# The order of VectorE's two groups of sums in the seven-product down projection

## The reference

```python
D_FF = 4 * D_MODEL          # 4096, D_MODEL = 1024, SEQ = 512, DEPTH = 2
h = rms_norm(x, g_mlp_pre)
f = jnp.square(jax.nn.relu(h @ w_up)) @ w_down
return x + rms_norm(f, g_mlp_post)
```

## Time and profile before

| | us |
|---|---|
| median of three runs | 2084.41 |
| lowest and highest | 2078.05, 2085.26 |
| the profiled execution's own time | 2079.13 |
| its span in the profile | 2077.0 |

### The profile page before, as it was taken

The page is one execution under the profiler, slowest core; times in us unless marked ns, Lnnn a source line. Parts: engine busy times, 40 slices in busy tenths (PEclk is TensorE's granted clock), DMA queues, the critical chain, the costliest instruction groups (busy, mean ns, idle before and its releaser), DMA issues.

```text
span 2077.0 us, 28000 instructions
## 1 busy us (share of the span) xinstructions
PE 2027.3 (98%) x10072; PEld 1626.9 (78%) x10072; DVE 1330.8 (64%) x1979; ACT 942.2 (45%) x1385; POOL 943.6 (45%) x368
## 2 busy tenths in 40 slices
PE   8999999999999999999999998999999999999999
PEld 7875888888888776888888886768776887888887
DVE  5866257787757654278778758884688624464555
ACT  6345464444453446543444452355576443333332
POOL 5433246544546233764666565224221353443442
PEclk9999999999999999999999999999999999999999
DMA  5432223333325331232333332232211332233222
GB/s 188 155 112 79 64 63 101 112 109 101 101 71 171 122 92 41 64 110 90 101 102 120 102 134 88 72 102 92 82 41 61 122 94 80 91 101 101 88 94 81
DMA packets 111854, 202.24 MB, mean 97 GB/s; under 512 B 6544, under 2 KB 51856, under 8 KB 111504
## 3 DMA queue, kind: packets, MB, share of 16 engines
q1 hardware_dynamic: 104800, 189.12, 28.2%
q10 hardware_dynamic: 6960, 11.88, 2.0%
HBM read 189.44 MB, written 8.12 MB: 95 GB/s over the span
## 4 chain that ended last, share of the span: by engine, by line
PE 73%; issue 16%; DVE 6%; POOL 4%; ACT 1%; DMA 0%; ACTq 0%; DVEq 0%; POOLq 0%
PE bank L800 40%; PE bank L1047 13%; PE bank L1027 7%; PE bank L914 5%; POOL w_lo L606 3%; PE bank L1058 2%; PE bank L925 1%; PE bank L872 1%; PE bank L983 1%; PE bank L943 1%; PE bank L971 1%; DVE partner L2728 0%; DVE w L2685 0%; POOL sums L622 0%; DVE pr L2299 0%
## 5 line engine op out<-in xcount | busy, mean ns | idle before, releaser
L606 POOL TENSOR_TENSOR w_lo<-raw,w_hi 128x2048 fp32r<-128x2048 f32 (+1 forms) x123 | 540.7, 4396 | 840.3 <-ACT w_hi L1547 825.8
L800 PE MATMUL bank<-act_hi,w_hi 128*128 128x512 f32 x1072 | 428.3, 400 | 5.2 <-POOL w_lo L606 2.7
L800 PE MATMUL bank<-act_hi,w_lo 128*128 128x512 f32 x1072 | 419.0, 391 | 0.0
L800 PE MATMUL bank<-act_lo,w_hi 128*128 128x512 f32 x1072 | 418.6, 391 | 0.0
L1547 ACT ACTIVATE w_hi<-raw 128x2048 fp32r<-128x2048 f32 (+1 forms) x112 | 203.2, 1815 | 266.3 <-PE bank L800 192.1
L800 PEld LDWEIGHTS bank<-act_hi,w_hi 128*128 128x128 f32 x1072 | 201.9, 188 | 58.8 <-issue 11.9
L800 PEld LDWEIGHTS bank<-act_hi,w_lo 128*128 128x128 f32 x1072 | 201.8, 188 | 43.2
L800 PEld LDWEIGHTS bank<-act_lo,w_hi 128*128 128x128 f32 x1072 | 202.0, 188 | 40.6 <-issue 1.0
L574 POOL TENSOR_TENSOR w_lo<-w_sum,w_hi 128x1024 fp32r<-128x1024 f32 x56 | 133.6, 2405 | 206.1 <-ACT w_hi L1856 192.6
L2562 DVE TENSOR_TENSOR f<-f,bank 128x512 f32<-128x512 f32 x196 | 133.3, 686 | 111.2 <-PE bank L1047 111.2
L1047 PE MATMUL bank<-w_hi,q_hi 128*128 128x512 f32 x392 | 152.7, 390 | 0.4 <-DVE w_lo L2569 0.4
(11 more groups left out here) (427 smaller groups left out, 4128.4 us busy)
## 6 DMA issues: line engine op xcount, KB each, us to landing
raw<-in_w_up SPq DMA_DIRECT2D x32, 1024.0 KB, 5.6
raw<-in_w_down SPq DMA_DIRECT2D x32, 1024.0 KB, 5.0
raw<-in_w_in SPq DMA_DIRECT2D x26, 1024.0 KB, 5.1
raw<-in_w_up SPq DMA_DIRECT2D x44, 512.0 KB, 4.5
raw<-in_w_in SPq DMA_DIRECT2D x28, 768.0 KB, 4.6
raw<-in_w_out SPq DMA_DIRECT2D x12, 1024.0 KB, 5.1
raw<-in_w_down SPq DMA_DIRECT2D x22, 512.0 KB, 4.2
raw<-in_w_attn_proj SPq DMA_DIRECT2D x4, 1024.0 KB, 5.1
```

The source lines that it names most:

```text
L606: pool.tensor_tensor(m.w_lo[slot][:, 0:n], m.raw[slot][:, 0:n], m.w_hi[slot][:, 0:n].bitcast(F32), ALU.subtract).then_inc(s["split_ready"], 1)
L800: mm = pe.matmul(o, ll if i == 2 else lh, rl if i == 1 else rh, start=first and n == 0, stop=last and n == len(steps) - 1)
```

## The change

`step` on VectorE calls `w_factors` ahead of `h_factors`. Nothing else differs: the same instructions, operands, semaphores and counts.

```diff
@@ -2562,8 +2562,8 @@
             dve.tensor_tensor(sums, sums, bank[b][:], ALU.add).then_inc(s[f"free{b}"], 1)
 
         def step(last=False):
+            w_factors()
             h_factors()
-            w_factors()
             for n in range(2):
                 wait("p_hi")
                 dve.tensor_tensor(half_slot(m.w_lo, n), quarter(m.raw[n], 0), half_slot(m.w_hi, n).bitcast(F32), ALU.subtract
```

## The result

The changed kernel takes 2174.86 us (median of four runs, 2174.65 to 2177.04) against 2081.23 for the kernel before on the same chip: ratio 1.0454, 95% interval 1.0440 to 1.0467, or 94 us more. The forecast was 2157, the range 2133 to 2178.

The account below looks back on a forecast made before the run. TensorE was taken as the bound, busy 263.98 of 264.00 us in the changed stretch. Waits with late first matmuls, 61 us, plus clock falls, 12, made 73 on 2084.4: 2157 us, range 2133 to 2178.

Parts of the forecast that it names:

- The chain of the step: Issue of the second down-weight half to first down matmul: 18.97 us, against 14.60 before in the second step.
- the pair of low parts: VectorE's activation work: the pair takes 1.30 us in place of 5.40, no longer beside GpSimd's copy.
- It does not heal: Across steps: everything upstream moves with TensorE, so each of 14 steps pays its wait anew.
- The rival of a second wait: `p_hi` or additions late behind the first wait: 1 to 2 us a step, 2171 to 2185 us; chance 0.07.
- The freed collision: GpSimd's copy beside an idle VectorE: load starts 0.1 us earlier at best, 1.4 us in all.
- not slower: Rival: relieved GpSimd copy lets the load issue early; 4.4 us per step to be found, time 2084; chance 0.04.
- The clock: TensorE behind each step's idle time: granted clock falls in 8 of 14 steps at 1.5 us, 12 us.
- every gap brings a fall: Rival on TensorE's clock: a fall in all 14 steps, 22 up to 38 us, 2168 to 2184; chance 0.14.
- the row of 10.2 us: Earlier trace: behind an idle 6.25 us, TensorE's clock stood at 0.50 for 10.2 us.
- The row at 1743.96: Earlier trace: behind an idle 2.72 us TensorE's clock stayed at 1.00, taken as showing a shorter gap does not pay.
- the forecast alone: The main case without rivals, with its own bounds: covers 2143 to 2168 us; chance 0.60.
- The slack: Second step: first down matmul could be ready at 348.23 but starts at 350.85, 2.6 us of slack.

Follow-up runs that it names:

- four more sums: The kernel before, order unchanged, with its first weight sum made four more times in front of the four: 2159.6 us, ratio 1.0371.
- two more sums: The kernel before, order unchanged, with its first weight sum made two more times in front of the four: 2100.23 us, ratio 1.0087.
- one sum ahead: The kernel before, with only the weight sum that needs the first half of the down weights ahead of the activation work: 2085.97 us, ratio 1.0040.
- sums in the middle: The changed kernel, with the weight sums moved behind the first two activation sums and low parts: 2099.23 us, ratio 1.0100.

## Why the prediction was right, and where it was wrong

**The chain of the step** held term by term. Landing and wake-up 5.0 (5.17 in the step shown), weight sums 5.12 (5.04), activation work 7.5 (7.44), start of the low part to matmul 1.35 (1.45); sum 18.97 against 18.61 to 19.11. Over 14 steps the distances grew by 58.7, forecast 59.5; at TensorE it is 57, because the issue itself comes 0.1 us earlier against it. With 1.5 for the first matmuls it is 59, where the forecast had 61. The largest correction, 5.40 less 1.30 for the pair of low parts, was right.

**It does not heal, and no second wait comes.** Each step paid anew. Between steps nothing else on TensorE was new, and `p_hi` cost nothing (ScalarE began its two at 359.11, 1 us each, and VectorE wanted the first at 361.16). The rival of a second wait is out. One small sum in this part is off: by the earlier trace rows the two `w_lo` end 2.36 - 1.35 = 1.01 us after TensorE's start and not 1.14. The changed kernel has `w_lo` and the four rectifications done 3.3 us after it, not 3.7, and nothing hangs on the difference.

**The freed collision** gave what the rows said: GpSimd's copy takes 4.61 in the changed kernel, 4.72 before, so the load was issued 0.1 earlier. The rival "not slower", which needed 4.4, is out.

**The clock** is the term that was mis-sized. The prediction had a fall in 8 of 14 steps at 1.5 us, 12 us in all. The fall came in 14 of 14, at 2.4 to 2.9 us in twelve and 1.6 in two, 35 us; so what happened is the rival "every gap brings a fall", priced 22 to 38 and given a chance of 0.14. Two things were wrong in the step. I set the chance of a fall halfway between an idle time of 2.72 without one and one of 6.25 with it, though the runs have now shown that an idle 2.0 us can bring it (seventh step with four more sums) and that none of 50 gaps of 3.4 us or more went without. And I took the price from a stretch of 3.5 us, though the row of 10.2 us said that a longer one is possible. The Trainium skill (TensorE: Matmul & The Clock Gate, Part 1) says that an idle array falls to 1.2 GHz and needs sustained work to come back. By that alone every gap would pay; the traces agree for the gaps of this change, 14 of 14, and not for the shorter ones of the other runs, of which 52 of 62 went without a fall. The row at 1743.96 that I held against it was one such case: with six matmuls in the gap, 9 of 14 idle times of at most 2.8 us went without a fall as well.

So the median lies within the range only because the range was widened for that rival; the forecast alone, with its bounds, ended at 2168. And part of the closeness in absolute time is luck: the kernel before took 2081.23 and not 2084.41 when it was measured again, so that the time was missed by 18 us, but the difference, 94 against 73, by 21.

**The slack** of 2.6 us in the second step is shown by the run with two more sums: 2.5 us vanish there in the second to seventh steps. In the second layer the same run shows 2.5 - 1.6 = 0.9 in four steps, which the prediction did not need and did not state, and which the expectation of one sum ahead then missed.

No version tried is faster than the kernel before. Its TensorE has no idle time in these steps but for 0.45 us, so the order on VectorE can only keep or lose what is there.

## What to carry to other kernels

An engine's instructions are a queue: a wait moved ahead of independent work holds that work too. Before an operation with a load behind it is moved forward, look in the trace for what now runs under that load, and price the move as landing plus all that is queued behind, less the slack at the engine that bounds. When that engine is TensorE, add the clock: a wait of 4 us cost 6.7 here, and 17 matmuls into a bank that is overwritten anyway brought the clock's share back. They fit the wait of this kernel, which is as long as they are; with more of them than the wait holds, which no run tried, the first product would come later.

## What the runs showed of the hardware that I had not expected

TensorE's granted clock against its idle time as the trace prints it, one gap per step, all runs of this case (steps without idle time are left out):

| idle time ahead of the first product | gaps | with a fall to 0.50 | length of the low stretch |
|---|---|---|---|
| 0.4 us or less (17 matmuls in the gap) | 14 | 0 | |
| 0.1 to 1.5 us (sums in the middle 14, two more sums 6, one sum ahead 5) | 25 | 0 | |
| 1.9 to 2.4 us (four more sums 6, two more sums 1, one sum ahead 1) | 8 | 4 | 3.4 us |
| at most 2.8 us, mean 2.5 (six matmuls in the gap) | 14 | 5 | 3.4 us |
| 2.9 us (two more sums) | 1 | 1 | 6.8 us |
| 3.4 to 5.5 us | 50 | 50 | 6.8 us in 41, 3.4 in 9 |

The 50 are 14 of the changed kernel, 14 of its repetition, 14 with the waits alone moved, and 8 with four more sums. The low stretch can begin while TensorE is still idle (at 361.10 in the second step, 1.5 us ahead of the first product at 362.61) and lasts into the work behind it.

GpSimd and VectorE side by side: VectorE's pair of low parts goes from 1.30 to 5.40 us beside GpSimd's copy, and the copy from 4.61 to 4.72. In this collision VectorE is held almost wholly. In the second step of the kernel before the copy starts first (331.29 against 331.76) and ends at 336.01, and the pair ends at 337.16, so that 1.15 us of its 1.30 of work were done behind the copy. GpSimd is not spared everywhere, though: its table operation `c_part` (line 676) takes 1.05 us in the changed kernel, where VectorE waits for its load, up to 1.51 in the kernel before, and 2.03 beside VectorE in the run with one sum ahead. VectorE's additions of line 2562, which have one input in a PSUM bank, are not held at all: all 196 take 673 to 689 ns, and 178 of them have GpSimd working beside them.
